# A float32r GEMM stream: its tiles cut at column 280, the high and low right parts in one 480-column matmul

## What is computed

```
x (520 x 1024)
layer 0:  h = rmsnorm(x) @ w_in0                (1024 x 2560)
          y = [ B * conv3(C * h'),  gelu(u) * (W_s rmsnorm(gelu(v)) + b) ] @ w_out0
layer 1:  q, kv, gates = rmsnorm(x) @ w_in1     (1024 x 2608)
          y = sparse attention (compressed, selected, window branches) @ w_out1
each:     x = x + y
          x = x + (silu(rmsnorm(x) @ w_a) * (rmsnorm(x) @ w_b)) @ w_ffn_out    (2816 wide)
at the end: rmsnorm(x); also the new k/v rows, the convolution states and v rows
```

## Time and profile before

| | |
|---|---|
| median of 3 runs | 1518.61 us (1515.12 to 1521.22) |
| span of the profiled execution | 1521.6 us |
| mean granted TensorE clock | 0.980 of full speed |
| TensorE matmul busy | 1469.1 us, 97% |
| VectorE / ScalarE / GpSimd busy | 577.0 / 484.7 / 515.6 us |
| DMA | 124.02 MB, 82 GB/s on average |

### The profile page before, as it was taken

The page is one execution under the profiler, slowest core; times in us unless marked ns, Lnnn a source line. Parts: engine busy times, 40 slices in busy tenths (PEclk is TensorE's granted clock), DMA queues, the critical chain, the costliest instruction groups (busy, mean ns, idle before and its releaser), DMA issues.

```text
span 1521.6 us, 26668 instructions
## 1 busy us (share of the span) xinstructions
PE 1469.1 (97%) x10754; PEld 1322.9 (87%) x10754; DVE 577.0 (38%) x985; ACT 484.7 (32%) x731; POOL 515.6 (34%) x136
## 2 busy tenths in 40 slices
PE   7997999999999999999898999999899999999998
PEld 6997999999999999999584445447799999999997
DVE  5347442222223333143556555552242222223232
ACT  5311342232232333112015556552233222223232
POOL 6422334334336555332201000000233443444652
PEclk9998999999999999999979999999899999999999
DMA  5221222332322333353610000006233223222332
GB/s 188 84 84 56 85 84 83 101 92 83 94 82 77 95 95 111 111 133 120 125 54 22 1 1 1 0 1 184 46 100 95 83 84 109 83 74 82 89 95 76
DMA packets 208062, 124.02 MB, mean 82 GB/s; under 512 B 30964, under 2 KB 205100, under 8 KB 207998
## 3 DMA queue, kind: packets, MB, share of 16 engines
q1 hardware_dynamic: 207998, 123.14, 27.6%
HBM read 117.75 MB, written 5.38 MB: 81 GB/s over the span
## 4 chain that ended last, share of the span: by engine, by line
PE 50%; issue 33%; POOL 10%; SPq 2%; DMA 2%; DVE 1%; ACT 1%; POOLq 0%; DVEq 0%; ACTq 0%
PE PG L430 31%; POOL WL L1632 10%; PE PG L974 5%; PE M L1020 5%; PE M L1008 3%; PE M L947 2%; DMA WBD<-in_w_cmp 1%; PE PG L958 1%; POOL SQX L1627 1%; DMA SLOT<-in_cache_win 1%; PE M L1120 1%; SPq L785 1%; PE M L908 1%; SPq L789 1%; SPq L790 0%
## 5 line engine op out<-in xcount | busy, mean ns | idle before, releaser
L1632 POOL TENSOR_TENSOR WL<-WR,WH 128x2048 fp32r<-128x2048 f32 x105 | 484.6, 4615 | 691.4 <-ACT WH L490 691.4
L430 PE MATMUL PG<-H,WH 128*128 128x260 f32 x4128 | 671.4, 285 | 18.7 <-DVE P L1855 11.0
L430 PEld LDWEIGHTS PG<-H,WH 128*128 128x128 f32 x4128 | 568.4, 190 | 21.3 <-DVE P L1855 11.4
L430 PE MATMUL PG<-H,WL 128*128 128x260 f32 x2064 | 417.5, 283 | 0.0
L430 PEld LDWEIGHTS PG<-H,WL 128*128 128x128 f32 x2064 | 319.7, 189 | 0.0
L430 PE MATMUL PG<-G,WH 128*128 128x260 f32 x1920 | 309.2, 283 | 1.5 <-DVE G L1392 1.5
L490 ACT ACTIVATE WH<-WR 128x2048 fp32r<-128x2048 f32 x105 | 200.4, 1908 | 275.5 <-PE PG L430 243.6
L430 PEld LDWEIGHTS PG<-G,WH 128*128 128x128 f32 x1920 | 263.7, 189 | 1.7 <-issue 1.7
L430 PE MATMUL PG<-G,WL 128*128 128x260 f32 x960 | 194.0, 283 | 0.0
L430 PEld LDWEIGHTS PG<-G,WL 128*128 128x128 f32 x960 | 148.5, 189 | 0.0
L607 DVE TENSOR_TENSOR TB<-PG,RSTD 128x520 f32<-128x520 f32 x44 | 30.8, 699 | 213.0 <-PE PG L430 213.0
(11 more groups left out here) (228 smaller groups left out, 1071.0 us busy)
## 6 DMA issues: line engine op xcount, KB each, us to landing
WR<-in_w_ffn_in SPq DMA_DIRECT2D x88, 512.0 KB, 4.6
WR<-in_w_in SPq DMA_DIRECT2D x32, 512.0 KB, 4.4
WR<-in_w_ffn_out SPq DMA_DIRECT2D x32, 384.0 KB, 3.8
WR<-in_w_ffn_out SPq DMA_DIRECT2D x32, 320.0 KB, 3.2
WR<-in_w_in SPq DMA_DIRECT2D x18, 256.0 KB, 3.5
WR<-in_w_out SPq DMA_DIRECT2D x8, 512.0 KB, 3.8
PST<-in_cache_kv SPq DMA_DIRECT2D x32, 128.0 KB, 2.1
WR<-in_w_out SPq DMA_DIRECT2D x16, 256.0 KB, 5.9
```

The source lines that it names most:

```text
L430: mm = pe.matmul(PG[:, par, hf, 0:HALF], w, x, start=(first and at_k == 0 and n == 0), stop=(last and at_k == nk - 1 and n == 2))
L1632: w_split.on(pool.tensor_tensor(WL[:, b, :], WR[:, b, :], WH[:, b, :].bitcast(F32), ALU.subtract))
```

## The change

The tile is no longer cut in the middle. Its left part is columns 0 to 279 (`CUT = 280`), its right part the other 240. The right part of the high tokens and that of the low tokens lie 520 numbers apart in H or G; one matmul with the high weights now streams both, 2 x 240 columns, and writes them side by side into one bank: the high product to columns 0 to 239 and the low product to 240 to 479. The left part moves to the end of its bank (from `TILE0 = 232`), so that the 520 sums are contiguous over both banks. The low product of the right part is thus kept apart in PSUM and added when the tile is drained. A k-step becomes five matmuls of 280, 280, 480, 280 and 240 columns.

```
-                for hf, n, w in ((0, 0, wh), (0, 1, wh), (1, 0, wh), (1, 1, wh), (0, 2, wl), (1, 2, wl)):
-                    cols = slice(hf * HALF, (hf + 1) * HALF)
-                    x = src[:, k0 + kk, 1 if n == 1 else 0, cols]
-                    mm = pe.matmul(PG[:, par, hf, 0:HALF], w, x, start=(first and at_k == 0 and n == 0),
-                                   stop=(last and at_k == nk - 1 and n == 2))
+                x, fresh, done = src[:, k0 + kk, :, :], first and at_k == 0, last and at_k == nk - 1
+                left, right = PG[:, par, 0, TILE0:512], PG[:, par, 1, 0:T - CUT]
+                both = PG[:, par, 1, 0:2 * (T - CUT)].rearrange("p (n c) -> p n c", n=2)
+                pe.matmul(left, wh, x[:, 0, 0:CUT], start=fresh, stop=False)
+                pe.matmul(left, wh, x[:, 1, 0:CUT], start=False, stop=False)
+                pe.matmul(both, wh, x[:, :, CUT:T], start=fresh, stop=False)
+                pe.matmul(left, wl, x[:, 0, 0:CUT], start=False, stop=done)
+                mm = pe.matmul(right, wl, x[:, 0, CUT:T], start=False, stop=done)
...
+        def drain_scaled(dve, par, dst, scale):
+
+            low_ok.on(dve.tensor_tensor(LOWT[:, par, :], lows(par), scale[:, CUT:T], ALU.mult))
+            low_ok.on(dve.tensor_tensor(dst, sets(par), scale, ALU.mult))
+            dve.wait_ge(low_ok.sem, low_ok.now)
+            tile_out.on(dve.tensor_tensor(dst[:, CUT:T], dst[:, CUT:T], LOWT[:, par, :], ALU.add))
...
-                    tile_out.on(dve.tensor_tensor(row(XT, m), row(XT, m), sets((U0[name] + c) % 2), ALU.add))
+                    low = XT[:, one(m), CUT:T].rearrange("p a c -> p (a c)")
+                    low_ok.on(dve.tensor_tensor(low, low, lows((U0[name] + c) % 2), ALU.add))
+                    dve.wait_ge(low_ok.sem, low_ok.now)
+                    tile_out.on(dve.tensor_tensor(row1(XT, m), row1(XT, m), sets((U0[name] + c) % 2), ALU.add))
...
-        lay = [16512]
+        lay = [2176]
-    nc = bacc.Bacc("TRN2", target_bir_lowering=False, num_devices=1)
+    nc = bacc.Bacc("TRN2", target_bir_lowering=False, num_devices=1, dynamic_dma_scratch_size=2048)
```

More of the change, by code:

```diff
@@ L22 @@
 HALF = T // 2
+CUT = 280
+TILE0 = 512 - CUT
 KD = D // P
@@ L181, in program @@
         GAINS = new("GAINS", [P, N_GAIN])
+        LOWT = new("LOWT", [P, 2, T - CUT])
         rstd_at = lay[0]
@@ L358, in sets, with lows @@
         def sets(par):
-            return PG[:, par, :, 0:HALF]
+            return PG[:, par, :, :].rearrange("p b c -> p (b c)")[:, TILE0:TILE0 + T]
+        def lows(par):
+            return PG[:, par, 1, T - CUT:2 * (T - CUT)]
         def halves(x):
@@ L556, in drain @@
                 dve.wait_ge(tile_done.sem, m + U0[name] + 1)
-                tile_out.on(dve.tensor_tensor(row(P0, m + first), sets((U0[name] + c) % 2), halves(RSTD[:, :]), ALU.mult))
-            with loop(dve, trips, [(tile_out, 4)]) as t:
+                drain_scaled(dve, (U0[name] + c) % 2, row1(P0, m + first), RSTD[:, :])
+            with loop(dve, trips, [(tile_out, 4), (low_ok, 8)]) as t:
                 for c in range(4):
@@ L564, in dve_residual @@
         def dve_residual(dve, name, i, gcol, per):
-            with loop(dve, KD // per, [(tile_out, per), (acc_ok, per)] + [(h_ready, per)] * (i < 4)) as t:
+            with loop(dve, KD // per, [(tile_out, per), (acc_ok, per), (low_ok, per)] + [(h_ready, per)] * (i < 4)) as t:
                 for c in range(per):
@@ L604, in body @@
                 dve.wait_ge(tile_done.sem, ua + 1)
-                tile_out.on(dve.tensor_tensor(halves(TA[:, j, :]), sets(U0[name] % 2), halves(RSTD[:, :]), ALU.mult))
+                drain_scaled(dve, U0[name] % 2, TA[:, j, :], RSTD[:, :])
                 dve.wait_ge(tile_done.sem, ua + 2)
-                tile_out.on(dve.tensor_tensor(halves(TB[:, :]), sets((U0[name] + 1) % 2), halves(RSTD[:, :]), ALU.mult))
+                drain_scaled(dve, (U0[name] + 1) % 2, TB[:, :], RSTD[:, :])
                 dve.wait_ge(a_silu.sem, m + KF * l + 1)
@@ L613, in body @@
                 g_ready.on(dve.tensor_tensor(row2(G, m, 1), TG[:, j, :], row2(G, m, 0).bitcast(F32), ALU.subtract))
-            with loop(dve, KF // 2, [(tile_out, 4), (t_gate, 2), (g_ready, 2)]) as t:
+            with loop(dve, KF // 2, [(tile_out, 4), (t_gate, 2), (g_ready, 2), (low_ok, 8)]) as t:
                 for j in range(2):
@@ L859, in rope_banks @@
         def rope_banks(r):
-            return M[:, 2:4, 0:HALF] if r < 4 else sets(r % 2)
+            return (M[:, 2:4] if r < 4 else PG[:, r % 2])[:, :, 0:HALF]
         def rope_pe(pe, r, m):
@@ L1164, in project @@
             dve.wait_ge(tile_done.sem, u + 1)
-            tile_out.on(dve.tensor_tensor(row(P0, m), sets(u % 2), halves(RSTD[:, :]), ALU.mult))
+            drain_scaled(dve, u % 2, row1(P0, m), RSTD[:, :])
         def prompt_ct(dve, kv):
@@ L1854, in in0_out @@
                 dve.wait_ge(tile_done.sem, u + 1)
-                tile_out.on(dve.tensor_tensor(halves(P0[:, 18 - u // 2 * 2 + u % 2, :]), sets(u % 2), halves(RSTD[:, :]),
-                                              ALU.mult))
+                drain_scaled(dve, u % 2, P0[:, 18 - u // 2 * 2 + u % 2, :], RSTD[:, :])
             def v_square(x):
@@ L1928, in conv_y @@
                 dve.wait_ge(vec.sem, vec.now)
-                tile_out.on(dve.tensor_tensor(halves(TG[:, x % 2, :]), sets(x % 2), halves(P0[:, 4 + FO[x], :]), ALU.mult))
+                drain_scaled(dve, x % 2, TG[:, x % 2, :], P0[:, 4 + FO[x], :])
                 dve.wait_ge(tile_out.sem, tile_out.now)
```

1 line of the change is left out of this document (added).

## The result

The changed kernel takes 1524.7 us (median of 7 runs, 1522.7 to 1528.0) beside 1513.8 us for the kernel before on the same chip (7 runs, 1513.1 to 1521.2). The ratio is 1.006, with an interval of 1.004 to 1.008: slower by 0.6%, about 9 us by the ratio, where 40 us less were forecast.

The account below looks back on a forecast made before the run. The kernel was taken as a stream of float32r matmuls on TensorE. -46.0 for k-steps, +2.4 norms, +0.3, +0.8 and +2.4 first projection gave -40 us: 1481.5 as a span, 1479 us forecast, range 1462 to 1514.

Parts of the forecast that it names:

- rival 2: Matmul stream: cost by the column or the page's rule, so only added drains or 4 us gained; 1522 to 1526, chance 0.10.
- a fixed charge: Matmul stream: 11.3 ns per float32r matmul whatever its width, so one fewer saves 0.011 us a k-step; 1510, chance 0.17.
- my floor: Matmul stream: a weight load holds each float32r matmul to at least about 119.7 ns; k-step 0.684 us, 0.034 less.
- The term of -46.0: Outside the first projection: 1352 k-steps, each 0.034 us shorter, save 46.0 us.
- The page's rule: Matmul stream: a warm matmul takes N/2.4 + 2.5 ns, so the change saves 2.5 ns a k-step, 4 us in all.
- The drains' length: VectorE's drains: the extra multiply adds 0.32 us and the add with its wait 0.45, +0.78 until the tile's release.
- After a norm: Both wide stages and the layer-1 projection: the first drain's added time is bare, about 0.8 us each, 2.4 in all.
- The first projection: VectorE is the bound there from about 102 us, so added drains cost net +2.4 us in place of -5.4.
- the rivals without a faster stream: First projection, forecasts where the matmul stream gains little or nothing: the added drains cost +3.1 or +3.5 us there.
- Wide and down stages hidden: Wide and down FFN stages: added drain time stays hidden, the first wide tile's stuck add by 0.8 us.
- inq, the rotation and the end: inq's first slot, already waiting for POOL, gives back 0.3 us; the rotation's first bank and the very end 0.4 each.
- Layout at nothing: Whole kernel: the 2 KB DMA scratch in place of 16 and the moved buffers cost nothing.

Follow-up runs that it names:

- w_f32r: Kernel before with each k-step's six matmuls made 512, 512, 64, 128, 192 and 256 columns wide, all float32r, for timing only: 233.5 ns at 512 columns.
- w_f32r_one: Kernel before with float32r matmuls of 512, 512, 64, 128, 192, 256 columns, one activation column repeated over the width, for timing only: 217 ns at 512.
- e2_onedrain: Changed kernel with each drain one operation again, the right part's low product computed but not added: 1515.6 us, 0.9993 of the kernel before.
- e3_nolock: Changed kernel with the low part copied to SBUF, added to the right part in PSUM, and the 520-wide multiply last: 1526.2 us, 1.0063 of the kernel before.
- e0_layout: Kernel before with only the change's memory layout: 2 KB DMA scratch, buffers moved down, an unused LOWT. 1518.5 us, 1.0 of the kernel before.

## Why the prediction was wrong, step by step

- **The step that failed: "I take it that a weight load sets a floor near 119.7 ns under each float32r matmul, and that columns count only above it."** It came from three rows: nothing beside the columns in the cold clock, 3 ns extra for the plain float32 matmuls, and 111 ns for one-column matmuls. The first doesn't tell a floor from a slower delivery by the column, because the second hides at 0.83 ns a column. I wrote that sentence myself, beside rival 2, and gave it 0.10. It doesn't exclude a fixed charge either, as I had it: the 2.5 ns of a bfloat16 matmul vanish at 1.2 GHz too (426.5 ns at 512 columns). And it spoke against my floor: in w_f32r the floor of the loads is 214 ns at 1.2 GHz, twice the 113, and a floor of 119.7 that doubles would have shown as 239 where 217 stand. The second was a comparison of another kind of operand. The third was the real floor, 111 to 113 ns, and I stretched it to 119.7 to close the gap. w_f32r and w_f32r_one show what stands in its place: 0.457 ns a column, which goes with the moving operand's row of 4-byte columns, and under it a floor of 111 to 113 ns, which a matmul of 260 columns is above. The 240 measured 110.3, not 119.7; the 280s 129.9, not 120.7; the 480 219.2, not 202.5. The term of -46.0 was +1.2 (0.9 ns x 1352).
- **The page's rule.** By the warm rule of the Trainium skill ("TensorE: Matmul & The Clock Gate", "Back-to-back issue gap"), which that section gives for a matmul by itself, 110.8 ns were due where 119.6 were measured. The bfloat16 runs meet it (216 at 512, 109.5 at 256), float32r rows don't (233.5). Its verdict, that the cut saves next to nothing and doesn't repay the drains, was the right one all the same.
- **The drains' length: right.** Multiply, multiply, add follow each other at 0.32, 0.72 and 0.4 us.
- **After a norm: right, a little too large.** 0.8 forecast, 0.6 to 0.7 measured (6.52 in place of 5.94 us; 6.65 in place of 5.94 in the layer-1 projection).
- **The first projection: right in kind, too small in size.** +2.4 forecast, +3.5 in the rivals without a faster stream; +8.75 measured, of which e2_onedrain gives 7.6 to the drains (1.5 of them through the clock behind a longer wait, a cost that the forecast had at nothing) and the executions' clock makes up the rest. I had let GpSimd's stops swallow part of the five drains. They swallowed nothing. Beside e2_onedrain, the tile starts that are 9.29, 8.60, 7.78, 11.84 and 8.09 us apart there are 10.04, 11.57, 8.54, 12.60 and 8.83 apart in the changed kernel: a whole drain's 0.75 four times, and 2.97 once. Here a stop was not shortened by what was put ahead of it; it caught the next operation with two SBUF operands. At 105.20 it caught L1882 for 4.26 us; now it catches the one before it, for 4.89:

```profile
107.28 4.89 DVE L1917 TENSOR_TENSOR TG<-P,TA 128x520 f32<-128x520 f32 x1
```

- **Wide and down stages hidden: right.** e3_nolock takes the stuck adds away and gains nothing. What the wide stages lost, 1.2 us each, is 0.6 at the tile after the norm, 0.07 at the next (5.82 in place of 5.75) and 1.6 ns at each of 352 k-steps.
- **inq, the rotation and the end: right in sign, too small, and one for another reason.** The +0.3 was for a faster stream running into GpSimd's WL. The stream wasn't faster, but the pause before inq's first matmul went from 1.2 us, ended by WL, to 1.6, ended by the new add, and inq's first tile from 8.07 to 8.84. For the rotation's first bank and the end +0.4 each were forecast; the waits went from 0.79 to 1.55 and from 1.2 to 1.9.
- **Layout at nothing: right** (e0_layout).
- **Rival 2 was the case**: 1522 to 1526 forecast, 1524.7 measured. It was met partly by luck: its +7 was short of the 9 by the ratio (4 of the 7.6 in in0 were missing), and the median before was 1513.8 in place of the 1518.6 that it started from.

What stays open is why a row of 4-byte columns comes at 0.457 ns a column in place of 0.417. w_f32r_one changes the addresses and the variety of the data at once, so a limit in the read and an effect of the data are not told apart. Open too is the small rest: why the uneven cuts take 3 and 6 ns a k-step more than the better of the two rules gives them.

## What to carry to other kernels

An excess over the ideal that vanishes in the slow clock may be a slower rate by the column, a floor that the clock leaves alone, or a small charge that only the fast clock shows; only a second width tells them apart, so let the forecast lean on none until one is measured. Before cutting matmuls differently, put the costs as the larger of columns and weight load: where every piece is above the floor, a cut is worth little (here between nothing and 6 ns in 720), and each piece under it costs. And price an added drain where the drain is waited for (here the first projection and the tiles behind a norm), not where its stall looks longest. Before comparing two profiles stage by stage, compare their granted clocks in that stage.

## What the runs showed of the hardware

- 4-byte weight loads of 128 columns hold a run of short matmuls to 113 ns each at 2.4 GHz and 214 at 1.2 GHz, loads of 64 columns to 58.5; 2-byte loads showed no such limit (a matmul of 128 columns took 57).
- At 512 columns float32r rows are taken at 0.456 ns a column, every second bfloat16 at 0.44, bfloat16 side by side and one repeated float32r column at 0.42. At 1.2 GHz float32r and bfloat16 alike take 427 ns, 0.83.
- A stream that changes between float32r and bfloat16 operands is slower than its parts: 735 ns a k-step with four changes and 708 to 710 with one, where 697 were due.
- VectorE's add with both operands in SBUF averaged 2863 ns beside GpSimd's work, and 417 with one in PSUM. The Trainium skill says the same ("SBUF — State Buffer", "Who interferes with whom"), and here it was true and cost nothing.
- Behind the same wait of 2.2 to 2.3 us TensorE's granted clock was 1.2 GHz for a stretch in e0_layout and e2_onedrain and stayed at 2.4 in the kernel before: 1.4 us between executions.
- The attention stage, the same work in both kernels, lasted 352.3 us at a mean granted clock of 0.95 in one execution and 338.5 at 0.98 in another.
